# First modulation in quarters of the features; ropes and inner attention steps of layer 1 placed inside other products

## The reference

```
silu_c, silu_cc = silu(c), silu(c_ctx)
for l in range(2):
    mod   = silu_c  @ w_mod[l] + b_mod[l]          # 6144 numbers: sh1, sc1, g1, sh2, sc2, g2
    mod_c = silu_cc @ w_mod[l] + b_mod[l]
    h  = rms_norm(x,   norm1[l]) * (1 + sc1)  + sh1
    hc = rms_norm(ctx, norm1[l]) * (1 + csc1) + csh1
    na_q, na_k, na_v, gq, gk, gv, ga, gb = split(h @ w_in[l])     # the same for hc
    ya = neighbourhood attention (8 heads, bias by table), window and context keys in one softmax
    q, k = rope(rms_norm(gq) * q_gain), rope(rms_norm(gk) * k_gain)
    yb = grouped attention (8 query heads, 2 key heads), keys of both sequences
    x  = x + g1 * ((sigmoid(ga) * (ya @ w_pa) + sigmoid(gb) * (yb @ w_pb)) @ w_o)
    ... (context likewise in layer 0), then a gated feed-forward with sh2, sc2, g2
```

## Time and profile before

| | us |
|---|---|
| median of 3 runs (lowest, highest) | 2476.87 (2474.17, 5926.69) |
| the profiled execution's own time | 2475.06 |
| its span in the trace | 2473.3 |
| TensorE busy in the span | 2418.5 |
| VectorE busy | 1558.7 |
| ScalarE busy | 1221.9 |
| GpSimd busy | 363.4 |
| mean granted clock of TensorE | 0.994 |

### The profile page before, as it was taken

How to read it: one execution, slowest core, us unless ns; L and a number is a source line. 1 busy time by engine, 2 the same in 40 slices (tenths; PEclk the granted TensorE clock), 3 DMA queues, 4 the chain that set the end, 5 groups by cost and what they waited for, 6 DMA issues and landing times.

```text
span 2473.3 us, 36743 instructions
## 1 busy us (share of the span) xinstructions
PE 2418.5 (98%) x14470; PEld 2060.2 (83%) x14470; DVE 1558.7 (63%) x2659; ACT 1221.9 (49%) x2224; POOL 363.4 (15%) x340
## 2 busy tenths in 40 slices
PE   8999999999999999999999999999999999999998
PEld 6765678878888777888888889998888888999887
DVE  5234455764455445677677768677767867757875
ACT  4344444322222435566556545466656654547653
POOL 0332422100001315200100000240010010024000
PEclk9999999999999999999999999999999999999999
DMA  6334323443444322345555553354555554335544
GB/s 275 129 110 155 128 96 134 141 167 130 167 161 144 148 86 86 139 169 182 176 209 188 175 168 132 135 178 178 180 189 188 180 192 151 133 115 202 188 171 136
DMA packets 88603, 390.05 MB, mean 158 GB/s; under 512 B 15024, under 2 KB 27600, under 8 KB 58352
## 3 DMA queue, kind: packets, MB, share of 16 engines
q1 hardware_dynamic: 81232, 356.17, 41.2%
q0 software_dynamic: 7200, 31.52, 3.6%
HBM read 386.62 MB, written 1.05 MB: 157 GB/s over the span
## 4 chain that ended last, share of the span: by engine, by line
PE 87%; DVE 5%; ACT 4%; DMA 2%; issue 1%; SPq 0%; POOL 0%; DVEq 0%; ACTq 0%; POOLq 0%
PE ps L1170 38%; PE ps L1210 37%; PE ps L1398 3%; PE ps L1475 2%; DVE ring_lo L2121 2%; PE ps L1460 2%; PE ps L1449 2%; DMA prob_t<-w_mod 1%; ACT w_hi L1624 1%; ACT logits L1857 1%; DMA ring<-w_w_in 1%; PE ps L1301 1%; PE ps L1316 1%; PE ps L1410 0%; ACT prob_t L1864 0%
## 5 line engine op out<-in xcount | busy, mean ns | idle before, releaser
L2121 DVE TENSOR_TENSOR ring_lo<-ring,w_hi 128x1024 fp32r<-128x1024 f32 (+4 forms) x708 | 773.3, 1121 | 232.9 <-ACT w_hi L1624 230.5
L1624 ACT ACTIVATE w_hi<-ring 128x1024 fp32r<-128x1024 f32 (+4 forms) x708 | 634.2, 944 | 268.9 <-PE ps L1170 177.4
L1170 PE MATMUL ps<-h_hi,w_hi 128*128 128x256 f32 (+1 forms) x1632 | 501.3, 333 | 2.7 <-issue 1.6
L1170 PE MATMUL ps<-h_lo,w_hi 128*128 128x256 f32 (+1 forms) x1632 | 488.9, 325 | 1.5 <-DVE h_lo L2294 1.5
L1210 PE MATMUL ps<-h_hi,w_hi 128*128 128x512 f32 x1760 | 447.0, 393 | 2.2 <-DVE h_hi L2294 1.8
L1210 PEld LDWEIGHTS ps<-h_hi,w_hi 128*128 128x128 f32 x1760 | 316.9, 189 | 58.8 <-issue 2.8
L1170 PEld LDWEIGHTS ps<-h_hi,w_hi 128*128 128x128 f32 x1632 | 308.5, 191 | 38.7 <-issue 11.9
L1170 PEld LDWEIGHTS ps<-h_lo,w_hi 128*128 128x128 f32 x1632 | 308.9, 191 | 26.2 <-DVE h_lo L2294 1.7
L1170 PE MATMUL ps<-h_hi,ring_lo 128*128 128x256 f32 (+1 forms) x1632 | 304.9, 324 | 2.5 <-DVE ring_lo L2121 2.5
L1170 PEld LDWEIGHTS ps<-h_hi,ring_lo 128*128 128x128 f32 x1632 | 250.3, 190 | 27.8 <-DVE ring_lo L2121 3.0
L1210 PEld LDWEIGHTS ps<-h_hi,ring_lo 128*128 128x128 f32 x1760 | 243.1, 191 | 21.4 <-DVE ring_lo L2121 3.5
(11 more groups left out here) (298 smaller groups left out, 2915.0 us busy)
## 6 DMA issues: line engine op xcount, KB each, us to landing
ring<-w_ffn_in SPq DMA_DIRECT2D x132, 1024.0 KB, 4.8
ring<-w_ffn_out SPq DMA_DIRECT2D x96, 704.0 KB, 4.0
ring<-w_in SPq DMA_DIRECT2D x36, 1024.0 KB, 4.8
ring<-w_w_in SPq DMA_DIRECT2D x26, 1024.0 KB, 4.9
bias_t<-w_mod POOLq DMA_DIRECT2D x24, 1024.0 KB, 5.3
ring<-w_mod SPq DMA_DIRECT2D x16, 1024.0 KB, 7.1
ring<-w_up SPq DMA_DIRECT2D x16, 576.0 KB, 3.7
ring<-w_pab SPq DMA_DIRECT2D x8, 1024.0 KB, 4.8
```

Of the source, the lines that this page charges most:

```text
L1170: mm = pe.matmul(ps[fs[k].bank][:, at_col:at_col + n], (hi_w if wpart == "hi" else lo_w)[0:rows, at[k]:at[k] + P], hi if part == "hi" else ...
L1624: act.activation(w_hi[q.s % 2][:, h * n:(h + 1) * n], ring[q.slot][:, h * n:(h + 1) * n], ACT.Copy)\
L2121: dve.tensor_tensor(ring_lo[q.slot][:, c], ring[q.slot][:, c], plain(w_hi[q.s % 2][:, c]), ALU.subtract)\
```

## The change

Two places change. **In the opening** the first modulation is computed in four quarters of the features, each with shift and scale side by side in one 512-column row. A quarter has two products (the two halves of the contraction), one row copy, one turn of four matmuls and one amplitude for two chunks. Each of its two buffers is filled by two DMAs that pick 256 of the 512 columns of four groups, so a contiguous piece is 1 KB. The first quarter's loads are issued before the two weight pieces, the other three behind them. The list is rewritten: rows follow for two chunks at a time, and the products of both tiles stand between the quarters. **In layer 1's first attention** the five ropes take banks of the linear turn and stand inside the token product, before its matmuls 4, 12, 20, 28 and 36. Items 0 and 1 share gate 0 (item 1 inside it, before matmul 12), items 2 to 14 have gates 1 to 13 behind them, items 15 and 16 share gate 14, items 17 and 18 share gate 15, and item 19 is alone.

```
-        def first_src(half, v_, k):
-            return w["mod"][0].rearrange("(u k) p n -> k p u n", k=2)[k][:, 2 * v_ + half, :].rearrange("p (u n) -> p u n", u=4)
+        def first_src(q, k, v_):
+            block = w["mod"][0].rearrange("(u k) p n -> k p u n", k=2)[k][:, 2 * v_ + q // 2, :]
+            return block.rearrange("p (u n) -> p u n", u=4)[:, :, q % 2 * S:(q % 2 + 1) * S]
...
+            return add("rope", block=block, need=need, tb=turned_by if block == 1 else turned_by2, inside=inside,
+                       chunks=[(b, a, low, linear() if inside else fill(T_BANKS[i % 2]), count("rope")) for i, (b, a, low) in enumerate(chunks)])
...
             add("first_squares")
-            mod_in(0, (0, 0), (0, 1))
+            mod_in(0)
             add("first_norm", n=n)
-            add("first_scaled", n=n, chunks=range(4))
-            mod_in(0, (1, 0), (1, 1))
+            split(0)
+            normal(0, 1)
             turn(0)
-            split(0)
             rows(0, 1)
             split(1)
+            parts(0, 0, 1)
+            normal(2, 3)
+            parts(1, 0)
+            mod_in(1)
+            parts(1, 1)
+            turn(1)
             rows(2, 3)
-            add("first_scaled", n=n, chunks=range(4, KC))
             split(2)
             split(3)
-            parts(0, 0, 1, 2)
-            mod_in(1, (0, 0), (0, 1))
-            parts(0, 3)
-            mod_in(1, (1, 0), (1, 1))
-            parts(1, 0)
-            turn(1)
-            parts(1, 1, 2, 3)
-            rows(4, 5, 6, 7)
-            parts(0, 4, 5, 6, 7)
-            parts(1, 4, 5, 6, 7)
+            parts(0, 2, 3)
+            for q in (2, 3):
+                normal(2 * q, 2 * q + 1)
+                mod_in(q)
+                parts(1, 2 * q - 2)
+                turn(q)
+                parts(1, 2 * q - 1)
+                rows(2 * q, 2 * q + 1)
+                parts(0, 2 * q, 2 * q + 1)
+            parts(1, 6, 7)
...
+                among = {4 + 8 * i: rope([r], 1, need=(hn["last"],), inside=True) for i, r in enumerate(ropes)}
                 tok("nav", w["w_nav"][l], 2, SLOT, 512, SQ, nav)
+                plan.items[-1]["mids"] = among
                 next(vals)
-                rope(ropes, 1, need=(hn["last"],))
...
+                def two_steps():
+                    att(g)
+                    att(g, inside=True)
+                    inside = g["last"]
+                    next(gates)
+                    plan.items[-1]["mids"] = {12: ("att", inside)}
+                two_steps()
+                for _ in range(13):
+                    att(g)
+                    next(gates)
+                two_steps()
+                two_steps()
             while g["i"] < len(g["steps"]) + 4:
                 att(g)
                 next(gates, None)
...
+            def first_mod(q):
+                for k in range(2):
+                    i = 2 * q + k
+                    for v_ in range(2):
+                        sp.dma_start(first_mod_in[i][:, 0:SLOT].rearrange("p (u v n) -> p u v n", u=4, v=2)[:, :, v_], first_src(q, k, v_))\
+                            .then_inc(first_landed[i], 16)
             first_mod(0)
             for p in plan.pieces:
                 if p.n == 2:
-                    first_mod(1)
+                    for q in range(1, 4):
+                        first_mod(q)
...
                                 for part in parts:
+                                    if at_mm in mids:
+                                        pe_rope(mids[at_mm])
+                                    at_mm += 1
```

More of the change, by code:

```diff
@@ L599, in att, with rope @@
                     g["last"] = add("att", steps=steps, i=i, inside=inside)
-        def rope(chunks, block, need=()):
-            add("rope", block=block, chunks=[(b, a, low, fill(T_BANKS[i % 2]), count("rope")) for i, (b, a, low) in enumerate(chunks)],
-                need=need, tb=turned_by if block == 1 else turned_by2)
+        def rope(chunks, block, need=(), inside=False):
+            return add("rope", block=block, need=need, tb=turned_by if block == 1 else turned_by2, inside=inside,
+                       chunks=[(b, a, low, linear() if inside else fill(T_BANKS[i % 2]), count("rope")) for i, (b, a, low) in enumerate(chunks)])
         def head_norm(chunks, sel, root, low=(0,) * 6):
@@ L630, in first_tiles, with mod_in, turn, normal @@
             count("sq_added", 0)
[L631 to L642 removed]
+            banks = [fill((MOD_BANK, TURN_BANK)[q % 2]) for q in range(4)]
+            turned = [fill(V_BANK) for _ in range(4)]
+            def mod_in(q):
+                for k in range(2):
+                    add("first_mod", q=q, k=k, f=banks[q])
+                add("first_row", q=q, f=banks[q])
+            def turn(q):
+                add("first_turn", q=q, of=banks[q], f=turned[q])
+                n["amp", q] = count("amp")
+            def normal(*chunks):
+                add("first_scaled", n=n, chunks=chunks)
             def split(j):
@@ L1278, in pe_first_turn @@
                 room(f)
-                for v_, of in enumerate(st["of"]):
-                    taken(of)
-                    for q in range(4):
-                        mm = pe.matmul(ps[f.bank][:, 8 * v_ + 2 * q:8 * v_ + 2 * q + 2], (row, spare)[v_][:, q * P:(q + 1) * P],
-                                       summed_sel[:, :], start=True, stop=True)
+                taken(st["of"])
+                for i in range(4):
+                    mm = pe.matmul(ps[f.bank][:, 2 * i:2 * i + 2], (row, spare)[st["q"] % 2][:, i * P:(i + 1) * P], summed_sel[:, :],
+                                   start=True, stop=True)
                 mm.then_inc(psum_full[f.bank], 1)
```

50 lines of the change are left out of this document (18 added, 32 removed).

## The result

The changed kernel took 2483.22 us, median of 11 runs (2477.88 to 2487.49), beside 2476.26 for the kernel before on the same chip (11 runs). The ratio is 1.0029, 95% interval 1.0020 to 1.0038: some 7 us slower, where 2477.3 and a range of 2473 to 2482.5 were forecast. About 1 us of the miss is the base: the forecast stands on the 2475.06 us of one execution, and the median of the kernel before is 2476.26. The interval is 0.1% to either side, so much less than the 2% of the prediction can be told apart here. The profiled execution shown here took 2478.91 us (span 2477.1, mean clock 0.992), so it is one of the quicker ones of its kernel.

What follows compares the result with a forecast made beforehand. TensorE, busy for 98% of the span, was taken as the bound. Opening +5.0 us and layer 1 -3.0 made +2.0 on one execution's 2475.06; the forecast was 2477.3 us, 8 in 10 between 2473 and 2482.5.

Steps and rivals of the forecast that it cites:

- Rival D: Opening: TensorE's new idling brings one or two more clock drops, 1.2 to 1.7 us each; 2479 to 2482; chance 0.1.
- The early start: Opening: the first quarter needs two loads, not four, so the first product comes at 22.6 us; 1.8 us saved.
- Rival B: Opening: small pieces load at 200 GB/s, making it 12.5 us longer and the time 2484.5; chance 0.1.
- (a): Opening: six modulation products lie behind the first product instead of four, about 1.0 us each; +2.0 us.
- (b): Opening: three turns of 8 instructions lie inside the stretch instead of one of 16; +0.85 us.
- (e): Opening: the DMA wait of 0.40 us before the last modulation product goes; -0.4 us.
- (c): Opening: TensorE waits for scaled rows behind each turn, 2.4 us at the second, 1.1 at the others; +4.0 us.
- (d): Opening: the third turn's row copy stands late in VectorE's queue, delaying that turn; +0.6 us.
- (f): Layer 1's attention: five ropes inside the token product cost 0.84 us each, no gain; bounds -1.0 and +1.0.
- (g): Layer 1's attention: five recurring waits of value products for the probability copies go; -2.1 us.
- (h): Layer 1's attention, end: half gates between steps 16 to 18 cut waits of 2.8 us to 0.7 and 0.5; -1.6 us.
- (i): Layer 1's attention: three steps inside a gate add three more switches to plain fp32 and back; +0.6 us.

Runs made afterwards that it cites:

- e6: The changed kernel with unread filler products in TensorE's waits, eight more ahead of the first product and six behind the second turn: 2482.54 us, ratio 1.0024.
- third trace: The changed kernel, unedited, run for a third trace of it: 2484.63 us.
- e11: The kernel before, unedited, run for a second trace of it: 2477.39 us.
- e7: The kernel before with only the five rope products of layer 1 moved inside the token product: 2479.01 us, ratio 1.0008.
- e8: The kernel before with only the attention's steps moved against the gates, three inside gates: 2473.89 us, ratio 0.9992.
- e2: The changed kernel's opening only, with layer 1's attention of the kernel before: 2484.60 us, ratio 1.0031.
- e5: The changed kernel with the opening's list reordered so that two ready products stand behind each turn: 2476.02 us, ratio 0.9996 to the kernel before.
- e9: The changed kernel with products reordered behind the turns and each quarter's load contiguous, 8 KB per partition: 2475.01 us, ratio 0.9996 to the kernel before.
- e10: The changed kernel with products reordered behind the turns and ten more unread products ahead of the first modulation product: 2474.16 us, ratio 0.9994.
- e4: The changed kernel with data laid out so each quarter's load is one 8 KB run per partition: 2483.87 us, ratio 1.0025.

## Why the prediction was wrong

**The step that failed** is the sentence "The lower clock at the first products I leave as it is", with bounds of -1.2 to +1.7 us. The change cost 2.3 to 2.5 us at equal clock, where the sum of the other steps said 2.0; the clock's part, by the correlation, was 3.3 to 3.7 us and was booked at nothing. It failed twice. In the opening, one stretch at 1.2 GHz that lay mostly over unread products became one or two among full-size products, one of them in all three traces at the new wait or within 1.3 us behind it (it begins at 36.1, 35.4 and 35.7 us); by e6 this cost 2.0 us in the trace. And the step looked at the opening only: more than half of the added low-clock time (5.1 of 9.1 us, by the means of the table, three traces against two) lies beyond 100 us, in places that the diff does not touch. Rival D, at chance 0.1 and 2479 to 2482, had the mechanism of the opening's part, and comes nearest; it had no term for the rest, and e6, which took the opening's part away, did not lower the median. So what makes most of the missing 3 to 4 us is known by its place and its company, low clock and late weight pieces, and not by its cause.

By its own steps, the opening:

- *The early start, -1.8:* came as -0.46, -1.0 and -1.2 in the three traces. The first load is used 0.7 to 1.4 us later (12.38 to 13.05 against 11.67), the second 1.2 to 1.9 later, for the pieces' 350 GB/s where 370 was taken and some delay of x itself (ScalarE begins on x at 9.55 in the first trace and at 8.99 and 8.86 in the others, against 8.73). Rival B, at 200 GB/s, is out. One of the prediction's own signs of being wrong, the loads landing after 16 us, came true narrowly and in the first trace only (second load used at 16.02, in the others at 15.48 and 15.32).
- *(a), (b) and (e):* six modulation products and turns inside. Summed from start to start in the first trace, the modulation grew from 4.32 to 5.56 us, +1.24 with the DMA wait gone (forecast +2.0 - 0.4); the turns' own time +0.73 (+0.85).
- *(c), the waits behind the turns, +4.0:* right in place and size. The idle columns of the first trace give 3.3 us against 0.61, which would be +2.7, but they count from modelled ends. From start to start, in the third trace, where the low clock begins only as the waits of the second turn end, the waits delay TensorE by 0.5 behind the first turn, 2.4 behind the second (2.4 forecast), and 1.0 and 0.9 behind the others (1.1 each), 4.7 in all against 0.8 before: +4.0. In the first trace it is +3.5, since low clock covers one of them.
- *(d), the late row copy, +0.6:* not seen; the third turn starts without a wait at 44.13.
- Left over is about 1 us inside the opening that no term had: e6 has +7.06 there at full clock (+6.55 with e11 as the base), the terms above make 6.0. The next block's first tile now waits for its weights' high part (0.20 us in the list, 0.36 from start to start), and the first pair behind every modulation product and turn takes 0.72 to 0.74 us and not 0.62, with more of these places than before; no run isolates them.

With 1.1 to 1.2 us of early start in e6, the opening is thus +5.5 to +5.8 at full clock against the forecast +5.2. That it is so near is in part luck: too much early start and a missing term of 1 us on one side, (d) and some 0.4 us too much for (a), (b) and (e) on the other.

Layer 1:

- *(f) ropes, 0 with bounds of 1.0:* -1.1 by e7's trace. A rope inside the token product costs 0.43 us (0.89 from 884.97 to 885.86, less two of the products' own spacings of 0.23), not 0.84. Of it 0.24 is the pair itself and 0.19 the slower product behind it, so the switches were sized rightly at 0.2 and the pair was not: the block's 0.64 was taken for it.
- *(g), (h), (i), -3.1:* -3.06 by e8's trace. The recurring waits went, by the steps and not by the ropes. At the end 1.21 and 0.99 are left, not 0.7 and 0.5, so (h) gave less, and the switches of (i) less too.
- Together -4.4 against -3.0, in the trace and at equal clock. By the median it is -3.3, the difference being what goes with the clock.

Rivals C (the opening costs nothing) and E (the edit does nothing) are out by e2 and the traces. The Trainium skill, "TensorE: Matmul & The Clock Gate", "What's actually happening", ties the gate to how busy the engine has recently been. The stretch at 36 us at the wait of 1.74 and those behind the long waits near 215 us agree with it; e5's 13.7 us at 1.2 GHz, in which TensorE was busy for 13.02, are hard to fit to it. That e6 filled the waits of the opening and its runs kept a mean clock of 0.9908 shows that the opening is not where most of the low clock comes from. The Trainium skill, "DMA: Bandwidth & Descriptors", Specifications, has line rate from 512 B up; the measured 350 GB/s in 1 KB pieces against 421 to 431 in 8 KB ones disagree, and the measurement decides.

**What stays open:** why the mean clock of the runs falls when only the opening (0.9924), only the ropes (0.9915) or both places (0.9910 and 0.9913) change, against 0.9935 before, 0.9931 for the steps and 0.9929 for the attention. The places of the stretches are nearly the same in all traces (near 189 to 235, 804 to 824, 866 to 882, 1053 to 1066, 1248 to 1275 us, and once at 145); whether one falls there and whether it is 3.4 us long or two or three times that differs between executions of one kernel. The late weight piece stands ahead of one of these places; whether an edit makes it later, or only chance does, fourteen traces do not tell (before 1.41 and 3.33 us of wait, changed 1.90, 4.19 and 3.01). The slope of 1.48 us is a correlation, and no run set the clock or the landing alone.

## What to carry to other kernels

When a chain of small steps is cut into more pieces, what counts is what TensorE has to do behind each piece: the same quarters cost 6 to 7 us less when two ready products stood behind each turn (e5) instead of one or none. Count a wait from start to start, not from the modelled end in the list; here that is 4.7 us against 3.3. In a kernel that TensorE bounds at 98%, price an idle microsecond with what it can do to the clock, and for changes of a few microseconds compare the runs' mean clocks beside their times: by the correlation half of this difference was there. And measure the halves of a combined change apart: here one was a gain of 3 us (2473.12) that the other, a loss of 8, hid. No opening in quarters came under it, the best ones (e5, e9, e10) included: 2474.16 to 2476.02.

## What the runs showed of the hardware that was not expected

- Loads in 1 KB pieces moved 347 to 355 GB/s where 8 KB ones moved 421 to 431, on the same queue at the same place of the program.
- The clock can stay at 1.2 GHz for 13.7 us on end at the start of a program, while TensorE is busy for 12.8 to 13.0 of them (e4, e5, e9).
- Going from fp32r to a fp32 pair of 256 columns and back inside a stream of products cost 0.43 us in all: 0.24 for the pair and 0.19 for the slower product behind it.
- A 1 MB weight piece issued at the same place of the program took 8.9 us to land in one execution and 11.2 in another of the same kernel, and TensorE's wait behind it went from 1.41 to 4.19 us over fourteen traces; a stretch at 1.2 GHz began about the end of the wait in eight of the nine traces with 2.47 us or more and in none of the five with less.
- Executions of one kernel on one chip spread by 7 to 11 us, and much of that goes with the printed mean clock, about 1.48 us for each 0.001.
